# Attention pairs: transposes for the next pair and row maxima moved by one to three steps, two of five divisions moved to another place

## The reference

```
q = rope_tail(rmsnorm(rmsnorm(h @ w_dq) @ w_uq))
k, v = mla_expand(ckv, kpe)          # sample keys also rotated, 128 cached keys appended
s = einsum('bqhd,bkhd->bhqk', q, k) * scale
o = softmax(s) @ v                   # then o @ w_o
```

## Time and profile before

| | |
|---|---|
| median of 3 runs | 3153.99 us (3151.72 to 3156.88) |
| the profiled execution's own time | 3155.11 us |
| its span, first to last instruction | 3153.0 us |
| mean granted TensorE clock | 0.968 |
| PE busy | 3011.7 us, 96% |
| PEld busy | 2884.9 us, 91% |
| DVE busy | 1491.0 us, 47% |
| ACT busy | 1001.6 us, 32% |
| POOL busy | 904.0 us, 29% |

### The profile page before, as it was taken

How to read it: one execution, slowest core, us unless ns; L and a number is a source line. 1 busy time by engine, 2 the same in 40 slices (tenths; PEclk the granted TensorE clock), 3 DMA queues, 4 the chain that set the end, 5 groups by cost and what they waited for, 6 DMA issues and landing times.

```text
span 3153.0 us, 43418 instructions
## 1 busy us (share of the span) xinstructions
PE 3011.7 (96%) x17065; PEld 2884.9 (91%) x17065; DVE 1491.0 (47%) x1825; ACT 1001.6 (32%) x1439; POOL 904.0 (29%) x573
## 2 busy tenths in 40 slices
PE   7999998999999999888999999998989999999999
PEld 7999998999999999787778888786989999999999
DVE  8445546456445554744566655566442222222222
ACT  3111213111111122323777677776222111121111
POOL 0221121112212121122665556666212112222111
PEclk7999998999999999897999999999989999999999
DMA  5222220222212221120000000000201111111112
GB/s 202 96 80 80 80 100 27 81 80 81 70 61 80 80 73 60 53 82 6 8 7 7 2 7 5 8 7 1 100 27 47 41 40 40 47 40 41 40 45 80
DMA packets 45539, 166.69 MB, mean 53 GB/s; under 512 B 5793, under 2 KB 7457, under 8 KB 45217
## 3 DMA queue, kind: packets, MB, share of 16 engines
q1 hardware_dynamic: 44912, 160.89, 15.0%
q10 hardware_dynamic: 560, 4.87, 0.4%
HBM read 156.15 MB, written 9.58 MB: 53 GB/s over the span
## 4 chain that ended last, share of the span: by engine, by line
PE 53%; issue 30%; POOL 14%; DVE 2%; ACT 1%; POOLq 0%; DVEq 0%; ACTq 0%
PE ps L907 52%; POOL p_lo L505 10%; POOL w_lo L489 2%; DVE x L1466 0%; POOL rot L516 0%; POOL q_tok L520 0%; DVE ps L1382 0%; POOL rot L514 0%; PE ps L1002 0%; PE ps L1212 0%; ACT tmp L592 0%; PE ps L996 0%; DVE tmp L1406 0%; POOLq L504 0%; DVE sums L1801 0%
## 5 line engine op out<-in xcount | busy, mean ns | idle before, releaser
L489 POOL TENSOR_TENSOR w_lo<-w_raw,w_hi 128x1024 fp32r<-128x1024 f32 (+2 forms) x190 | 465.2, 2449 | 1884.3 <-ACT w_hi L585 1884.3
L907 PE MATMUL ps<-h_hi,w_hi 128*128 128x384 f32 x2640 | 606.8, 337 | 37.7 <-DVE h_lo L1447 20.2
L907 PE MATMUL ps<-h_lo,w_hi 128*128 128x384 f32 x2640 | 603.3, 336 | 0.0
L907 PE MATMUL ps<-h_hi,w_lo 128*128 128x384 f32 x2640 | 602.6, 336 | 0.0
L907 PEld LDWEIGHTS ps<-h_hi,w_hi 128*128 128x128 f32 x2640 | 473.7, 190 | 42.4 <-issue 29.8
L585 ACT ACTIVATE w_hi<-w_raw 128x1024 fp32r<-128x1024 f32 (+2 forms) x190 | 194.7, 1025 | 956.7 <-PE ps L907 860.9
L907 PEld LDWEIGHTS ps<-h_lo,w_hi 128*128 128x128 f32 x2640 | 474.3, 189 | 0.0
L907 PEld LDWEIGHTS ps<-h_hi,w_lo 128*128 128x128 f32 x2640 | 473.6, 189 | 0.0
L505 POOL TENSOR_TENSOR p_lo<-p,p_hi 128x512 fp32r<-128x512 f32 (+1 forms) x304 | 389.8, 1294 | 257.2 <-ACT p_hi L830 253.3
L1466 DVE SCALAR_TENSOR_TENSOR x<-ps,mod,x 128x256 f32<-128x256 f32 (+5 forms) x432 | 240.2, 612 | 457.9 <-PE ps L907 456.9
L907 PE MATMUL ps<-hid_hi,w_hi 128*128 128x384 f32 x1536 | 348.8, 334 | 0.5 <-DVE x L1466 0.5
(11 more groups left out here) (142 smaller groups left out, 3551.4 us busy)
## 6 DMA issues: line engine op xcount, KB each, us to landing
w_raw<-in_wall_dram SPq DMA_DIRECT2D x174, 512.0 KB, 3.7
mod_raw<-in_mod_rows_dram SPq DMA_DIRECT2D x80, 512.0 KB, 3.6
x<-in_x_t_dram SPq DMA_DIRECT2D x8, 576.0 KB, 8.4
x_spill<-x ACTq DMA_DIRECT2D x1, 4608.0 KB, 13.8
x<-x_spill SPq DMA_DIRECT2D x1, 4608.0 KB, 13.5
out_dram<-x SPq DMA_DIRECT2D x8, 576.0 KB, 2.8
mod_shift<-in_mod_cols_dram SPq DMA_DIRECT2D x8, 512.0 KB, 14.5
mod_scale<-in_scale_rows_dram SPq DMA_DIRECT2D x8, 512.0 KB, 16.6
```

Source lines behind the costliest of these rows:

```text
L489: pool.tensor_tensor(w_lo[s][:, 0:words], w_raw[s][:, 0:words], w_hi[s][:, 0:words].bitcast(F32), ALU.subtract).then_inc(w_lo_done, 1)
L907: ins = pe.matmul(out, lhs[a], rhs[b](cols), start=first and n == 0, stop=last and n == 2)
```

## The change

Constants: the next pair's queries are turned after step 17 and its keys after step 19 (before, 20 and 21); head two's maxima start at step 1 instead of 0 and its rows are turned after step 14 instead of 13; the next pair's maxima start at step 22 instead of 23 and are turned after step 34 instead of 35. ScalarE drains the turned queries at step 20 and the keys at step 22 of its count. On VectorE, `over_sums` pieces 0 and 1 go from the next pair's front part to the end of their own pair, behind its last `max_rows` (pairs one to seven); piece 2 goes from behind the first key unit to behind query unit 3; and the last part of `token_scale` goes from ahead of head two's `max_rows` to behind it. The eighth pair does piece 2 of the pair before in its front part, and no longer 0 and 1. Outputs of head one stay at steps 25 and 26.

```diff
-TURN_A = STEPS + 1
-MAX_B, MAX_A = 0, TURN_A + 3
+TURN_Q, TURN_K = STEPS - 2, STEPS
+MAX_B, MAX_A = 1, TURN_K + 3
 ROWS_B, ROWS_A = MAX_B + 13, MAX_A + 12
...
-                        if pos == TURN_A + LAG and not last:
+                        if pos == TURN_Q + LAG and not last:
                             turn_part(U_V + U_TURN + U_QK + U_MAX, False)
-                        if pos == TURN_A + LAG + 1 and not last:
+                        if pos == TURN_K + LAG and not last:
                             turn_part(U_V + U_TURN + U_QK + U_MAX, True)
...
-                        if pos in (TURN_A + 5, TURN_A + 6):
-                            output(0, pos - TURN_A - 4, p)
+                        if pos in (STEPS + 6, STEPS + 7):
+                            output(0, pos - STEPS - 5, p)
...
-                            if pos in (TURN_A, TURN_A + 1):
-                                turn_part(k, pos > TURN_A)
+                            if pos in (TURN_Q, TURN_K):
+                                turn_part(k, pos == TURN_K)
...
-                def k_units(k, before=None):
+                def k_units(k):
                     for i, (a, z) in enumerate(groups(KTILES, 4)):
                         unit_sums(k + i, 2 * NT + 2 * a, 2 * (z - a), NOPE)
-                        if i == 0 and before is not None:
-                            over_sums(2, before)
...
                     for i in (3, 4):
                         q_unit(k + 3 + i, i)
-                        if before is not None:
-                            over_sums(i - 3, before)
-                    k_units(k + 8, before)
+                        if i == 3 and before is not None:
+                            over_sums(2, before)
+                    k_units(k + 8)
...
-                def pair(first, last, before):
+                def pair(first, last, p, before):
 
                     value_and_turn()
                     if not last:
-                        expand_and_turn(2 * U_V, before if not first else None)
+                        expand_and_turn(2 * U_V, before)
                     else:
                         for i in range(3):
                             turn_keys(2 * U_V + i, 1, i)
-                        for piece in range(3):
-                            over_sums(piece, before)
+                        over_sums(2, before)
                     for t in range(NT):
                         max_out(t)
-                        if not last and t >= 2:
+                        if not last and 2 <= t < NT - 1:
                             token_scale(t - 2)
                     max_rows(U_V + U_TURN + U_QK, 1)
+                    if not last:
+                        token_scale(NT - 3)
                     if not first:
                         for piece in range(3, 5):
                             over_sums(piece, before)
...
                         max_rows(U_V + U_TURN + U_QK + U_MAX + U_TURN, 0)
+                        for piece in range(2):
+                            over_sums(piece, p)
```

More of the change, by code:

```diff
@@ L1841, in _ @@
                 max_rows(U_QK + U_TURN, 0)
-                pair(True, False, None)
+                pair(True, False, 0, None)
                 with dve.Fori(1, PAIRS - 1) as p:
@@ L1845, in _ @@
                     S.enter(p - 1, n=5 + 1)
-                    pair(False, False, p - 1)
+                    pair(False, False, p, p - 1)
                     S.leave(PAIRS - 2)
@@ L1850, in high_row @@
                     dve.tensor_copy(h_hi[:, j, :], o32[:, j, :]).then_inc(h_hi_done, 1)
-                pair(False, True, PAIRS - 2)
+                pair(False, True, PAIRS - 1, PAIRS - 2)
                 dve.wait_ge(sums_used, 3 * PAIRS)
```

## The result

The changed kernel takes 3126.11 us (median of 4 runs, 3123.84 to 3129.35), the kernel before 3154.15 in the same comparison: a ratio of 0.9908, 95% interval 0.9897 to 0.992, or 28 us less. The profiled execution took 3127.27 us, 27.84 less than the one before.

What follows compares the result with a forecast made beforehand. TensorE's own work plus its waits was taken as the bound. Gains of 1.9 + 5.0 + 2.7 + 16.2 + 8 = 33.8 us took the profiled 3155.11 to 3121.3; median 1.1 lower, so 3120, range 3110 to 3135.

Steps and rivals of the forecast that it cites:

- Two divisions leave the expansion: Before scores 5: wait for sums of squares goes, 1.1 us for the exponential remains; fifth pair's way 7.69 to 5.0.
- The slow clock: TensorE's stretches at 1.2 GHz, 1.44 us a pair, go with the long wait; rival that they return: 3130, 14%.
- The rule of the Trainium skill: At the exponential's table load: a drain of about 1.38 us per set change, some 10 us less gain; not followed.
- Scores 19: Start of head two's scores: 1.8 us left behind the row maxima's transpose; wait 0 to 0.3, taken as 0.1.
- Keys and values 24: Keys' transposes wait 0.5 us for VectorE; values 24 wait 0.5 for GpSimd's weight split and low halves.
- The step that failed: Pair's end: 1.4 us of work covers tile nine's 0.36 wait, 0.70 covers the turned rows' 0.46; both waits go.
- Divisions 0 and 1 at the end of the pair: 4.5 us, up to 6.9, fall into VectorE's 5.45 us idle before the next first value drain; costed at nothing.
- The eighth pair: Last pair: shorter waits before tiles 0 and 1 and a better clock, together 5.7 to 8.7 us; taken as 8.
- the new waits did come: Rival, no new wait but the exponential's: the 1.1 us per pair charged for others go; 3113, 14%.
- the load did follow the root: Rival, ScalarE's exponential load is no earlier: it stays 0.56 us behind the square root, seven times; 3124, 5%.
- The queries' low halves did stand behind division 4: Slower rival: turned queries run into VectorE's divisions, keys wait 1.7 us, values 24 another 0.8, clock falls; 3160, 4%.
- nothing moves: Rival: ScalarE and GpSimd set the pace and TensorE's waits only change places; 3148 to 3156, 5%.

Runs made afterwards that it cites:

- half a step: Head two's maxima started half a step sooner, rows turned after step 13: on the changed kernel 3126.39 us; on it with four exponential buffers 3105.25 us.

## Why the prediction was right, and where not

The forecast was 3120 and the time 3126.11. The sum of 33.8 us came out as 30.76 in the attention of the profiled execution; that execution also reached its attention 2.84 us later (1463.54 for 1460.70), with nothing changed ahead of it. So of the 6 us that the forecast missed, 3 are the attention's, and the rest lies ahead of it, where nothing was changed. By pairs, predicted and measured: first 1.9 and 0.85; second 5.0 and 4.48; third 2.7 and 2.17; fourth to seventh 16.2 and 13.6; eighth 8 and 9.7.

- *Two divisions leave the expansion.* Right in mechanism and size. The exponential's load starts 0.01 us behind the root, the wait before scores 5 is 1.05 (1.1 forecast, though the forecast's own 4.4 less 3.4 is 1.0), and the way of 5.0 is 4.46 with tile 1 (0.6) behind it. The divisions alone do it, with 5.0 us; the later maxima alone do most of it too (5.24, with tile 1 behind). What held ScalarE is shown by the run of before with four buffers: the ring, by 1.45 us in the fifth pair.
- *The slow clock.* Its price of 1.44 us about holds: with four buffers the kernel before still has one such pair, and it takes 93.81 us where the next takes 92.27, which is 1.54. That it would go with the wait held for the change. That the wait is what brings it did not hold in general (last section).
- *The rule of the Trainium skill* ("ScalarE: Activation LUTs", "What ACT_TABLE_LOAD costs"). The load takes 1.28 us, as the page says. Its drain of some 1.38 us for a change of set is again not in the trace: 0.01 us lies between root and load, and as much between load and exponential. What I missed was another matter of tables: the root's own load ends 0.64 us after the sums are there. The sum is unharmed, as I took the root's time from the first pair, where this load stood in the way by the same 0.64.
- *Scores 19.* The place was right (1.8 behind the transpose; measured 1.79), the wait not: 0.54 for 0.1. I took the 3.23 us of before as all work, but some 0.6 of it was TensorE standing; with four buffers the kernel before takes 2.5 there. The sum is unharmed, since that stall went when the new one came.
- *Keys and values 24.* 0.35 and 0.56 for 0.5 and 0.5. But the price of values 24 does not hang on the weight split's place alone: split after step 8, it comes back at values 28. Four buffers remove it with the split where it was, and the keys' 0.35 as well, so it is the small lead that three buffers leave.
- *The step that failed.* "The last tile of the maxima gets scores 36 and values 33 ahead of it [...] Both go." They went, and 0.97 us at values 36 came in their place, which I had not charged: values 33 free the buffer of step 36's exponential (1928.13, held 0.71 by TensorE), and its low half, 1.27 us from 1929.47, ends 0.06 ahead of values 36. Before, the eighth tile (0.53), which now stands ahead of values 33, and the wait for the ninth (0.37) filled that time. TensorE in the fifth pair, values 33, tile nine and values 36 of before, then values 33 of the change:

```profile
1937.94 0.39 PE L907 MATMUL ps<-p_hi,v_hi 128*128 128x512 f32 x1
...
1940.78 0.33 PE L1212 MATMUL ps<-kT_hi,qT_hi 96*128 96x128 f32 x1 [0.37 <-DVE row_max L1783]
...
1941.70 0.48 PE L907 MATMUL ps<-p_hi,v_hi 128*128 128x512 f32 x1
```

```profile
1927.17 0.40 PE L907 MATMUL ps<-p_hi,v_hi 128*128 128x512 f32 x1
```

  From values 33 to values 36 it took 3.76 us before and takes 3.63 after the change (values 36 at 1930.80), so that only 0.13 was gained there; with four buffers it takes 2.88. Seven waits of 0.97 are 6.8 us. The attention's sum fell short by 3.0 only, since the eighth pair gained 1.7 more than taken and the ways to scores 19 and to the keys cost some 0.3 a pair less than charged.
- *The first pair* was costed like the others less the divisions 3 and 4; it has the 0.97 as well.
- *Divisions 0 and 1 at the end of the pair* cost nothing, as said: VectorE's idle time ahead of the first value drain is 2.64 us where it was 5.45. The 0.29 that I took for a product left alone is of 128 columns; one of 256 takes 0.42 (from 1932.61 here), so the worst case was 6.6 us and not 6.9.
- *The eighth pair* gained 1.7 more than taken, but its 9.7 lies a little above the 5.7 to 8.7 worked out. Its clock came back to 1.00, and TensorE's busy time fell by some 4 us where up to 3 had been taken; the waits ahead of tiles 0 and 1 fell by 5.2.

The rivals: the slow clock did not return; the new waits did come; the load did follow the root. The queries' low halves did stand behind division 4, which ended at 1901.09 in the fifth pair, but at a price of 0.35 and not 1.7. Of "nothing moves" one part was true: ScalarE and GpSimd, with three buffers, took back the 0.97 at values 36. The divisions alone, at 3131.69, lie within the range of 3110 to 3135 already; the range says little of the other parts.

## What to carry to other kernels

When a long wait goes, look for the shortest ring of buffers on the path behind it: here three buffers for the exponentials cost 1.9 us a pair after the change, and on the kernel before four gave 21.3 us of attention, the clock's share included, more than any one part of the change but the divisions (23.6). Try each part of a combined change alone and left out, since two parts may remove the same wait: the later maxima give 11.7 us alone and 0.4 on top of the others. A gain ahead of a floor is worth little until the floor is lifted: half a step was worth 0.2 us a pair with three buffers and 0.6 with four.

## What the runs showed of the hardware that was not expected

The same wait brings the slow clock in one pair and not in another. Stretches of 18 us around the wait, TensorE alone (length, busy, count, granted clock): third and fifth pair of before, then second and fifth pair of before with four buffers:

```profile
1677.36:1695.36 18.00, 15.96 (x110) 1.00 0.00 0
...
1866.11:1884.11 18.00, 16.08 (x104) 0.91 0.00 0
```

```profile
1584.94:1602.94 18.00, 16.07 (x104) 0.91 0.00 0
...
1863.07:1881.07 18.00, 16.08 (x111) 1.00 0.00 0
```

The wait is 1.9 us in all four, the busy time ahead of it alike, and the clock falls to the lower level in two. Two waits of 0.69 and 1.04 close together did it as well, in one pair of the kernel with the later maxima alone, and not in its five others:

```profile
1580.24:1598.24 18.00, 16.60 (x105) 0.91 0.00 0
1674.98:1692.98 18.00, 16.61 (x112) 1.00 0.00 0
```

What decides it stays open. No fall was seen in the middle pairs of the change and of the runs built on it; what they share is that TensorE stands no longer than some 1.1 us at once, which is not shown to be the reason: neither of the two waits above was longer.
